# One narrow matmul more ahead of each item of the up product of a mixture-of-experts kernel

## What is computed

```python
cap = EC_FACTOR * L // N_EXPERTS                       # 256 tokens for each of 16 experts
gate, idx = lax.top_k(jnp.swapaxes(aff, 1, 2), cap)
xs = h[bidx, idx]
hid = jax.nn.silu(jnp.einsum('becd,edf->becf', xs, w1)) * jnp.einsum('becd,edf->becf', xs, w3)
y = jnp.einsum('becf,efd->becd', hid, w2) * gate[..., None].astype(h.dtype)
return jnp.zeros_like(h).at[bidx, idx].add(y)
```

## Time and profile before

| what | us |
|---|---|
| two runs, median | 2154.77 and 2157.2, 2155.98 |
| the profiled execution, whole | 2155.14 |
| its span | 2153.4 |
| TensorE busy | 2074.0 (96%) |
| TensorE weight loads busy | 1813.9 (84%) |
| VectorE busy | 1370.2 (64%) |
| ScalarE busy | 996.3 (46%) |
| GpSimd busy | 278.0 (13%) |

### The profile page before, as it was taken

One profiled execution on the slowest core, in us unless ns is written; L12 is line 12 of the kernel. 1 busy time (PEld: TensorE's weight loads), 2 busy tenths in 40 slices (PEclk: granted clock), 3 DMA queues, 4 the chain that ended last, 5 costly groups with the idle time before them and its releaser, 6 DMA issues.

```text
span 2153.4 us, 35090 instructions
## 1 busy us (share of the span) xinstructions
PE 2074.0 (96%) x13569; PEld 1813.9 (84%) x13569; DVE 1370.2 (64%) x2082; ACT 996.3 (46%) x1630; POOL 278.0 (13%) x357
## 2 busy tenths in 40 slices
PE   6999999999999899997999999999999999999996
PEld 4778888888878677785999999999999999999985
DVE  3564548995994577757555656556555665656557
ACT  5923454444531445431444544445444444444455
POOL 0001100100001010020011112111221112111120
PEclk9999999999999999998999999999999999999998
DMA  7464333333327665456356666576565765657565
GB/s 258 150 240 136 112 107 99 114 113 94 125 76 237 235 209 178 144 213 257 118 207 243 218 217 208 190 259 214 196 218 191 273 203 186 216 214 258 196 230 225
DMA packets 188285, 407.95 MB, mean 189 GB/s; under 512 B 15956, under 2 KB 53396, under 8 KB 187300
## 3 DMA queue, kind: packets, MB, share of 16 engines
q1 hardware_dynamic: 162212, 318.36, 42.6%
q0 software_dynamic: 25984, 88.39, 12.6%
HBM read 329.59 MB, written 77.12 MB: 189 GB/s over the span
## 4 chain that ended last, share of the span: by engine, by line
PE 81%; DVE 10%; issue 3%; DMA 3%; ACT 2%; SPq 1%; POOL 0%; DVEq 0%; ACTq 0%; POOLq 0%
PE bh L55 11%; PE bh L57 11%; PE bh L56 11%; PE bank L55 8%; PE bank L57 8%; PE bank L56 8%; PE eby L55 5%; PE eby L57 5%; PE eby L56 5%; DVE acc L854 3%; PE ebt L2286 1%; PE bank L1037 1%; PE bank L1419 1%; DVE over L2018 1%; DVE raw L2474 1%
## 5 line engine op out<-in xcount | busy, mean ns | idle before, releaser
L55 PE MATMUL bh<-xt_hi,shi 128*128 128x256 f32 x2048 | 572.0, 279 | 3.0 <-DVE slo L2438 2.4
L56 PE MATMUL bh<-xt_lo,shi 128*128 128x256 f32 x2048 | 571.7, 279 | 0.0
L57 PE MATMUL bh<-xt_hi,slo 128*128 128x256 f32 x2048 | 571.7, 279 | 0.0
L2438 DVE TENSOR_TENSOR slo<-raw,shi 128x1024 fp32r<-128x1024 f32 x384 | 455.9, 1221 | 157.1 <-ACT shi L2348 153.0
L2348 ACT ACTIVATE shi<-raw 128x1024 fp32r<-128x1024 f32 x384 | 389.9, 1053 | 129.0 <-PE eby L57 127.2
L55 PEld LDWEIGHTS bh<-xt_hi,shi 128*128 128x128 f32 x2048 | 385.7, 188 | 4.2 <-issue 2.0
L56 PEld LDWEIGHTS bh<-xt_lo,shi 128*128 128x128 f32 x2048 | 385.8, 188 | 0.6
L57 PEld LDWEIGHTS bh<-xt_hi,slo 128*128 128x128 f32 x2048 | 385.8, 188 | 0.0
L55 PE MATMUL bank<-h_hi,whi 128*128 128x512 f32 x704 | 283.3, 402 | 0.0
L57 PE MATMUL bank<-h_hi,wlo 128*128 128x512 f32 x704 | 275.9, 392 | 0.0
L56 PE MATMUL bank<-h_lo,whi 128*128 128x512 f32 x704 | 275.7, 392 | 0.0
(11 more groups left out here) (347 smaller groups left out, 3121.7 us busy)
## 6 DMA issues: line engine op xcount, KB each, us to landing
raw<-in_exp_w_dram SPq DMA_DIRECT2D x96, 2048.0 KB, 11.1
uT<-stage POOLq DMA_DIRECT2D x72, 256.0 KB, 2.8
xb<-in_ada_w_dram SPq DMA_DIRECT2D x24, 512.0 KB, 6.0
wraw<-in_w_in_dram SPq DMA_DIRECT2D x22, 512.0 KB, 5.0
adaw<-in_ada_w_dram SPq DMA_DIRECT2D x8, 1024.0 KB, 10.1
xb<-in_x_dram SPq DMA_DIRECT2D x16, 512.0 KB, 4.4
xt<-in_x_dram POOLq DMA_DIRECT2D x16, 512.0 KB, 5.4
x2d<-xt POOLq DMA_DIRECT2D x16, 512.0 KB, 3.1
```

Source lines behind the costliest of these rows:

```text
L55: nc.tensor.matmul(out, w_hi, x_hi, start=start, stop=False)
L56: nc.tensor.matmul(out, w_hi, x_lo, start=False, stop=False)
L57: return nc.tensor.matmul(out, w_lo, x_hi, start=False, stop=stop)
L2438: nc.vector.tensor_tensor(item_dst(slo, n), item_src(n), item_dst(shi, n), ALU.subtract).then_inc(S["w_lo_ready"], 1)
```

## The change

In front of the 24 matmuls of every up item, and behind the item's wait, stands one more matmul. Its weights are the item's first 128 x 128 block in shi, the same as those of the L55 matmul that follows it. Its moving operand is the first `width` tokens of block 0 of xt_hi, where width is 64 for item 0, grows by 8 with each item and is 184 for item 15. Its output goes to the start of the bank ebt 0, where nothing reads it: the transposes for the next expert write that bank later. The operands lie as those of L55 do, the weights at 0 and the tokens at 32 modulo 256 bytes.

```diff
     NI, NR = 24, 4
+    FIRST_STEP, STEP = 64, 8
     FD = KD
...
                         for m in range(2):
                             n = 2 * f + m
                             pe.wait_ge(S["w_lo_ready"], e * NI + (n + 1))
+                            width = FIRST_STEP + STEP * n
+                            nc.tensor.matmul(bt[0][:, 0:width], shi[n % NR][:, 0:P], xt_hi[:, 0, 0:width], start=True, stop=True)
                             for k in range(KD):
```

## The result

The changed kernel takes 2187.32 us (two runs, 2187.31 and 2187.33) against 2155.98 us before: a ratio of 1.0145, with a 95% interval of 1.0102 to 1.0189. It is slower by about 31 us, less than the 2% that count here as a difference. The forecast was 2184 us, with a range of 2176 to 2196.

The account below looks back on a forecast made before the run. TensorE's matmul queue was taken as the bound for 15 of 16 experts. 247 added matmuls on the path x 0.114 us = 28.2 us, on the median 2155.98 giving 2184 us, range 2176 to 2196.

Parts of the forecast that it names:

- What bounds the kernel: Experts before the last: TensorE's matmul rate sets the time, with one wait of 0.6 us, so added queue work is paid in full.
- No new wait, and a clock that stays up: Added matmul in each up item: it waits for nothing new, delays no other engine, and TensorE's clock stays up.
- The load behind as the price: Up product: the next matmul's weight load sets each added matmul's price, 0.114 us, with 0.112 as floor whatever the width.
- like plain float32: Rival at the added matmul: narrow fp32r needs plain float32's passes, 0.216 us each, 53.4 us in all, 2209; chance 10%.
- the hidden load: Rival at the added matmul: weight loads run ahead or beside, 0.055 us each, 13.6 us, 2170; hidden or partly hidden 7%.
- the transposes' 0.034 us of mutual slowing: Rival at the added matmul: two four-byte streams slow each other, 0.146 us each, 36.1 us, 2192; chance 11%.
- 240 x 0.114: Experts before the last: all 240 added matmuls are on the path, at 0.114 us each.
- the case of 0.12 to 0.16 us: Added matmul: operand streams slow each other, so each costs 0.12 to 0.16 us; chance 11%.
- that of 0.110 to 0.120 with 72%: Added matmul: the weight load is the bound, each costs 0.110 to 0.120 us, likeliest 2182.5 to 2186; chance 72%.
- wide matmuls slower than 0.117 us: Sign against the forecast: in the up product, wide matmuls behind an added one start more than 0.117 us apart.
- an expert longer by more than its added matmuls: Sign against the forecast: a middle expert above the expected 69.9 us would point to a wait that had been ruled out.
- The seven matmuls of the last expert: Last expert: 7 of 16 added matmuls count, four before the silu at 2072.29 us and some three after 2097 us.

## Why the prediction was right, and where it was off

**What bounds the kernel** was right: TensorE has no wait in the middle experts, before or after, and each added nanosecond in its queue was paid.

**No new wait, and a clock that stays up** was right: the granted clock is 1.00 in the middle experts, and the waits are as before or shorter. But the prediction put the clock at no price. In the last expert it was down for 16 matmuls before, at 0.98 in the mean of the expert, and it is no longer.

**The load behind as the price** was right, and is the step on which the forecast stood. The single-column sums at L976, another type in another stage, gave 0.112 us; measured were 0.112 to 0.119 for the added one (over the pair with the wide one behind it), flat from 16 to 256 columns. The rival "like plain float32" (2209 us) fell with the run of 184 columns, the hidden load with every run, and the transposes' 0.034 us of mutual slowing did not appear.

**The size** was off. The term "240 x 0.114" came out as 240 x 0.129 = 31.0 us instead of 27.4. The mistake is the sentence that a narrower matmul "should not cost more than the wide one of the same kind". It does, by 0.008 to 0.021 us at 16 to 184 columns with fp32r weights of 128 columns, because it also changes how the 24 matmuls behind it keep in step. By its price per matmul, 0.129 us, the outcome belongs to the case of 0.12 to 0.16 us, which had a chance of 11%, and not to that of 0.110 to 0.120 with 72%. The prediction listed wide matmuls slower than 0.117 us as a sign against itself, which is what happened in 9 of 16 items; and it said that an expert longer by more than its added matmuls would point to a wait. It was longer by 0.2 us, and there was no wait.

**The seven matmuls of the last expert** were wrong in part: 0.8 us were forecast. The first four are there, with 0.5 us at the silu and 0.3 to 0.5 at the load of rows. The other three are not. The chain of before goes back to TensorE at 2097 us, but not for three items of work: from 2097.36 to the silu at 2104.79 us it passes two, and in the first of them 16 matmuls ran at half the clock after TensorE had waited, so that it took 1.6 us longer. With the added matmuls there is no such stretch, and the end comes 0.4 us earlier after the landing of the rows instead of 0.3 later. A stretch of a chain is no price for what is added in it, if another path is nearly as long, and less so if it holds a clock that the change brings back.

The three deviations are +3.6 us in experts 0 to 14, -1.8 in the last one (1.0 less instead of 0.8 more) and +2.2 of spread ahead of them. They add up to 4.0 us, the distance from the forecast 28.2 to the 32.2 between the profiles. Of the last expert's 1.0 us less, 0.4 are the clock and 1.0 a shorter load of rows, against 0.3 for the four matmuls; the load's part is luck. The forecast landed within 0.2% of the median because the second deviation took back half of the first, and because the median of before lies 0.8 us above the profiled run from which the other numbers come.

## What to carry to other kernels

In a row of matmuls like these each one has to cover the weight load of the one behind it. With 128 x 128 float32 or fp32r weights that was 0.112 to 0.117 us, so that a matmul of 16 columns cost as much as one of 256, and cutting columns saved nothing; only shorter loads behind it did. To price a matmul, take distances between starts, over a pair where a narrow one is followed by a wide one, and prefer the weight loads' rows. In a stage that consists of thousands of equal matmuls, 1 ns on each counts as much as the thing added: look at the distance of its neighbours, and at where their operands start in SBUF. And before a chain is read as work, look at the granted clock of its stretches: two items of TensorE looked like three here.

## What the runs showed of the hardware that was not expected

- A single narrow matmul sets the rhythm of the next 24: 116.7 or 117.7 to 117.9 ns on average, the second as a repeated 116, 118, 119, until the next disturbance. A matmul of 256 columns, like its neighbours, never did it. In one run a whole up product of 384 equal matmuls went at 117.8 with none added.
- With the tokens at 0 instead of 32 modulo 256 bytes behind weights at 0, each fp32r matmul of 256 columns takes 120.0 ns instead of 116.7, and the same disturbance then makes the next nine or so followers faster, 119.3 to 119.5 ns in the mean of an item.
- A 512-column matmul among 256-column ones costs 0.246 us, 0.019 more than the 0.227 that it costs among its like. Some 0.013 of these may be the rhythm behind it (117.8 instead of 116.7 ns for 24 matmuls in every second item); the rest was not taken apart.
- After TensorE had waited 0.66 and 1.78 us within 8.3 us, its granted clock fell to 0.5 and 16 matmuls of 256 columns took 0.213 us each instead of 0.117. With waits of 1.14, 0.24 and 0.14 us it stayed at 1.00.
- A bf16 matmul of 64 columns in a row of such costs 0.030 us, and 0.131 in front of a load of fp32r weights.
